# A transformer-like double block on one core: putting the square of each residual tile right behind its add

## The reference, cut to what matters

```python
y = jnp.concatenate([y_ssm, y_fft, y_att], axis=-1) @ w_out[l]
x = x + gt_m * rms_norm(y, g_post_mix[l])          # end of part 1
h = rms_norm(x, g_pre_ffn[l]) * (1.0 + sc_f) + sh_f
up = dwconv3(h @ w_up[l], conv_w[l], conv_b[l])
gate, val = jnp.split(up, 2, axis=-1)
y = (jax.nn.gelu(gate) * val) @ w_down[l]
x = x + gt_f * rms_norm(y, g_post_ffn[l])          # end of part 2
...
mix = jnp.einsum("btd,de->bte", merged, w_out[l])
h = h + rms_norm_2(mix, norm_mix_post[l])          # end of part 4
u = rms_norm_2(h, norm_mlp_pre[l])
hid = jnp.square(jax.nn.relu(jnp.einsum("btd,df->btf", u, w_up[l])))
m = jnp.einsum("btf,fd->btd", hid, w_down[l])
h = h + rms_norm_2(m, norm_mlp_post[l])            # end of part 5
```

## Time and profile before

| | |
|---|---|
| median of 3 runs | 2967.43 us (2966.15 to 2967.44) |
| the profiled execution | 2966.15 us |
| its span, first to last instruction | 2964.3 us |
| lies around the span | 1.85 us |
| PE busy | 2799.2 us (94%) |
| DVE, ACT, POOL busy | 1261.5, 875.9, 881.5 us |
| mean granted clock of TensorE | 0.97 of full speed |
| DMA | 246.00 MB, mean 83 GB/s |

### The profile page before, as it was taken

How to read it: one execution, slowest core, us unless ns; L and a number is a source line. 1 busy time by engine, 2 the same in 40 slices (tenths; PEclk the granted TensorE clock), 3 DMA queues, 4 the chain that set the end, 5 groups by cost and what they waited for, 6 DMA issues and landing times.

```text
span 2964.3 us, 31495 instructions
## 1 busy us (share of the span) xinstructions
PE 2799.2 (94%) x13134; PEld 2168.8 (73%) x13134; DVE 1261.5 (43%) x1580; ACT 875.9 (30%) x1312; POOL 881.5 (30%) x413
## 2 busy tenths in 40 slices
PE   6788889999999999979999999999999999999996
PEld 3656646778888888757777777677677888888885
DVE  6646622666444353463757522222553111111115
ACT  4413643432212121233545321111344111222112
POOL 1421113334333343333212111111245433333234
PEclk8999989999999999989999999999999999999998
DMA  6453245311111111223112221111322111111113
GB/s 229 172 143 107 59 172 209 116 55 57 43 50 50 50 43 50 100 86 114 50 57 96 76 72 54 48 59 54 121 92 105 59 43 50 50 50 43 50 50 135
DMA packets 86431, 246.00 MB, mean 83 GB/s; under 512 B 10769, under 2 KB 25617, under 8 KB 86289
## 3 DMA queue, kind: packets, MB, share of 16 engines
q1 hardware_dynamic: 78256, 219.25, 21.6%
q10 hardware_dynamic: 4608, 14.92, 1.3%
q0 software_dynamic: 3424, 9.81, 0.9%
HBM read 206.87 MB, written 37.07 MB: 82 GB/s over the span
## 4 chain that ended last, share of the span: by engine, by line
PE 82%; DVE 8%; ACT 3%; issue 2%; DMA 2%; POOL 2%; SPq 1%; ACTq 0%; POOLq 0%; DVEq 0%
PE ps L1309 24%; PE ps L1311 23%; PE ps L1310 23%; PE pc L1665 3%; PE pss L1615 1%; PE ps L1526 1%; PE ps L1472 1%; PE ps L1347 1%; POOL whl L2844 1%; PE pss L1278 1%; DMA adaw<-in_w_ada 1%; DVE y L1683 1%; DVE pad L1689 1%; DVE pad L1683 1%; POOL hid L2844 1%
## 5 line engine op out<-in xcount | busy, mean ns | idle before, releaser
L2844 POOL TENSOR_TENSOR whl<-wraw,whl 128x1024 fp32r<-128x1024 f32 (+1 forms) x247 | 640.3, 2594 | 1628.6 <-ACT whl L2402 1628.3
L1309 PE MATMUL ps<-act,whl 128*128 128x512 f32 x2464 | 1001.3, 406 | 48.0 <-DVE act L1683 11.8
L1311 PE MATMUL ps<-act,whl 128*128 128x512 f32 x2464 | 972.0, 394 | 0.0
L1310 PE MATMUL ps<-act,whl 128*128 128x512 f32 x2464 | 971.6, 394 | 0.0
L1309 PEld LDWEIGHTS ps<-act,whl 128*128 128x128 f32 x2464 | 468.2, 190 | 192.3 <-issue 75.1
L1310 PEld LDWEIGHTS ps<-act,whl 128*128 128x128 f32 x2464 | 469.1, 190 | 104.5 <-issue 8.6
L1311 PEld LDWEIGHTS ps<-act,whl 128*128 128x128 f32 x2464 | 467.6, 190 | 103.7
L2402 ACT ACTIVATE whl<-wraw 128x1024 fp32r<-128x1024 f32 (+1 forms) x247 | 256.4, 1039 | 432.2 <-PE ps L1311 393.6
L1309 PE MATMUL ps<-hid,whl 128*128 128x512 f32 x864 | 341.4, 395 | 5.4 <-POOL hid L2844 5.4
L1310 PE MATMUL ps<-hid,whl 128*128 128x512 f32 x864 | 338.4, 392 | 0.0
L1311 PE MATMUL ps<-hid,whl 128*128 128x512 f32 x864 | 338.3, 392 | 0.0
(11 more groups left out here) (321 smaller groups left out, 2461.9 us busy)
## 6 DMA issues: line engine op xcount, KB each, us to landing
wraw<-in_w_in SPq DMA_DIRECT2D x63, 512.0 KB, 3.5
wraw<-in_f1u SPq DMA_DIRECT2D x47, 512.0 KB, 3.5
wraw<-in_f2d SPq DMA_DIRECT2D x36, 512.0 KB, 3.5
wraw<-in_f2u SPq DMA_DIRECT2D x35, 512.0 KB, 3.4
wraw<-in_w_out SPq DMA_DIRECT2D x32, 512.0 KB, 3.5
x<-in_w_ada SPq DMA_DIRECT2D x32, 512.0 KB, 6.4
xs<-y SPq DMA_DIRECT2D x24, 512.0 KB, 6.7
x<-in_xT ACTq DMA_DIRECT2D x16, 512.0 KB, 8.6
```

The source lines that it names most:

```text
L1309: pe.matmul(PSB[g.bank][:, :], hi, src[:, 0, k, c], start=e == 0, stop=False)
L1310: pe.matmul(PSB[g.bank][:, :], hi, src[:, 1, k, c], start=False, stop=False)
L1311: m = pe.matmul(PSB[g.bank][:, :], lo, src[:, 0, k, c], start=False, stop=e == len(ks) - 1)
L2844: return g_.tensor_tensor(out, a, b, op)
```

## The change

It rewrites the loop in `residual`. Before, in half 0 the square of tile j was queued one turn after its add, the sum of tile j two turns after it, and a turn was 3.2 us of the plan's clock (2.0 the last of nine). Now the square is queued right behind its add, the sum one turn later, and a turn is 2.2 us (eight turns). In half 1 and for s = 5 the list stays as it was. No instruction is added or removed.

```diff
+        sums = []
+        for j in range(8):
+            p.put("r_add", s, half, j)
+            if final:
                 p.put("r_store", s, half, j)
                 yield 1.4
+                continue
+            b, free = p.use_sq(s, ("np", "rows2", s, half, j) if half else ("raS", s, j))
+            p.put("r_sq", s, half, j, b, free)
+            if half:
+                sums.append((j, b))
+            else:
+                p.sums.append((s, half, j, b))
+            if j:
+                p.add_sums(lambda entry: entry[2] < j)
+            yield 1.8 if half else 2.2
+            if len(sums) > 1:
+                p.put("r_sum", s, half, *sums.pop(0))
+        if final:
             return
-        sums = []
-        for j in range(9):
-            if j < 8:
-                p.put("r_add", s, half, j)
-            if half and j < 8:
-                b, free = p.use_sq(s, ("np", "rows2", s, half, j))
-                p.put("r_sq", s, half, j, b, free)
-                sums.append((j, b))
-                yield 1.8
-                if j:
-                    p.put("r_sum", s, half, *sums.pop(0))
-            elif half == 0:
-                if j:
-                    b, free = p.use_sq(s, ("raS", s, j - 1))
-                    p.put("r_sq", s, half, j - 1, b, free)
-                    p.sums.append((s, half, j - 1, b))
-                p.add_sums(lambda entry: entry[2] < j - 1)
-                yield 3.2 if j < 8 else 2.0
```

More of the change, by code:

```diff
@@ L628, in residual @@
         yield 1.2
-        if final:
-            for j in range(8):
-                p.put("r_add", s, half, j)
+        sums = []
+        for j in range(8):
+            p.put("r_add", s, half, j)
+            if final:
                 p.put("r_store", s, half, j)
                 yield 1.4
-            return
-        sums = []
-        for j in range(9):
-            if j < 8:
-                p.put("r_add", s, half, j)
-            if half and j < 8:
-                b, free = p.use_sq(s, ("np", "rows2", s, half, j))
-                p.put("r_sq", s, half, j, b, free)
-                sums.append((j, b))
-                yield 1.8
-                if j:
-                    p.put("r_sum", s, half, *sums.pop(0))
-            elif half == 0:
-                if j:
-                    b, free = p.use_sq(s, ("raS", s, j - 1))
-                    p.put("r_sq", s, half, j - 1, b, free)
-                    p.sums.append((s, half, j - 1, b))
-                p.add_sums(lambda entry: entry[2] < j - 1)
-                yield 3.2 if j < 8 else 2.0
+                continue
[11 more added lines that the diff above has]
+        if final:
+            return
         yield 1.0
```

## The result

The changed kernel takes 2990.42 us in the median (2983.91 to 2992.25, 4 runs), the kernel before 2967.43 (2966.15 to 2967.63, 4 runs): the ratio is 1.0075, with an interval of 1.0057 to 1.0092. It is slower by 0.75%. The profiled execution took 2984.79 us, 18.6 more than the 2966.15 of before; the forecast was 2984 with 17.8 more. The median lies inside the stated range of 2966 to 2993 and 0.4 us above the 2980 to 2990 that had most of the chance.

The account below looks back on a forecast made before the run. PE, busy 94% of the span, was taken as the bound. Two out-projections at +10.7 us each (+21.4) and -3.6 at s = 2 gave +17.8 on 2966.15: 2984 us, most likely 2980 to 2990, range 2966 to 2993.

Parts of the forecast that it names:

- The first stall: In each out-projection, PE arrives at `r_rows2` at 537.4 and waits 7.6 us for DVE's running sum, ready at 545.0.
- The clock behind it: After PE resumes at 545.0, `r_rows2` and two steps run at the low clock, 5.3 us allowed before `r_bc2` starts.
- The second stall: At `r_rows` of half 1 in each out-projection, PE waits 6 us for the last `nadd`, queued behind `apply`.
- the second has the same list: The out-projection at s = 4 was taken to cost the same 10.7 us as that at s = 1.
- the 2.1 us for the clock behind the second stall: Low clock at `r_rows` of half 1: 0.9 us more for it and 0.6 for each of two steps, per out-projection.
- The end of the first feed-forward: At s = 2, the last sum comes 5.9 us earlier, `diag` is held by POOL's split, and `r_bc2` gains 3.6 us.
- the 17.1 us wait shrinks to 11: Sign of a right forecast: PE's wait for DVE's `ss` sum at s = 2 falls from 17.1 to 11 us.
- R1: Rival, chance 0.10: DVE keeps up in the out-projections, the sum is ready at 537.8, the first stall vanishes; 2961 us.
- R2: Rival, chance 0.13: one stall only per out-projection; `r_rows` of half 1 comes at 563, +2.7 us each; 2968 us.
- R3: Rival, chance 0.15: ACT answers faster, the sum comes at 541, each out-projection costs 4 us less; 2976 us.
- R4: Rival, chance 0.07: full clock price, both out-projections at the upper bound of +15.5 us, no gain at s = 2; 2997 us.
- Part C: Half 1 and s = 5 keep their order, PE never waits for weights despite later splits: cost 0, else some 2 us.

## Why the prediction was right

**The first stall.** Forecast 7.6 us, measured 7.30 in both out-projections. The step that carried it was the walk of DVE's and ACT's new lists, round by round, and its round of 7.85 us was measured at 7.84. The other walk that might have been made is the plan's: turns of 2.2 us, sum ready in time. It fails since the plan's clock counts only PE's steps and knows of no queue.

What I had not separated is that two causes meet. The faster turn would have brought the sum 2.3 us forward, the new order loses that again, and PE's place moves by 7.5. The runs with one part each show it. The expectation of a later run, that the order alone would do no harm, was wrong: it costs 7 us at the old pace.

**The clock behind it.** I took `r_rows2` and two steps at the low level. The trace has `r_rows2` (1.87 us) and 4 steps, and `r_bc2` starts 8.5 us after `r_rows2`, not 7.3. This is the main part of the 1.2 us by which s = 1 came out above the forecast. At s = 4 it is 7.3, as forecast.

**The second stall.** At s = 1 the walk from `r_bc2` to the end of the last `nadd` gave 16.5 us (552.35 to 568.9), and measured are 16.4 (552.43 to 568.87). The stall is 5.9 where I had 6. At s = 4 it is 3.7. Here the step "the second has the same list" was too short: the order is the same, but `apply` has other instructions there. In the trace DVE writes the low parts as a plain TENSOR_TENSOR of 0.69 us, and POOL makes half of them, and from `r_bc2` (2219.47) to the end of that `nadd` (2233.82) it takes 14.3 us. That is not the whole of s = 4: `r_rows` of half 1 came 6.7 us later there instead of 8.6, and behind it the stretch lost 3.3 us more instead of 2.1. So the 2.1 us for the clock behind the second stall were too small, in both out-projections (2.4 at s = 1).

That the sum of the stretches is right to 0.2 us is luck: +1.2, -0.8 and -0.7 nearly cancel. The mechanism is not luck: both stalls came where they were said to, for the reason given, and three of the four came at their size. The fourth, the second stall at s = 4, is 3.7 us instead of 6.

**The end of the first feed-forward.** The last sum was forecast 5.9 us earlier. From `r_rows` to `r_rows2` it was 48.91 us and is 43.00: 5.91. Then `diag` was held, as walked, and `r_bc2` gained 3.55 where I had 3.6; the whole stretch gained 4.3. The sign "the 17.1 us wait shrinks to 11" did not come: it is 7.0 us, because PE came late, as told with PE's waits above; the sum came no earlier than forecast. The row of `diag` carries the price:

```profile
1332.23 2.62 DVE L1679 TENSOR_TENSOR diag<-ident,rcol 128x512 f32<-128x512 f32 x1
```

The Trainium skill (SBUF — State Buffer, "Who interferes with whom") has a DVE instruction with two SBUF inputs and a GpSimd instruction that reads SBUF shut each other out for the whole of an instruction. The trace agrees here too: 2.62 us against 0.69 in the kernel before. The half splits agree as well, since the add was let go with the first half (1.38 us).

**The rivals.** R1 (DVE keeps up) fell: the splits kept meeting the adds, and when the adds were taken away they met the sums. R2 fell with the second stall: `r_rows` of half 1 came 9.5 and 6.7 us later and not 2.7. R3, with the sum some 4 us earlier, fell with the first stall of 7.3 us. R4 fell on both counts: the out-projections cost 11.9 and 9.9 us and not 15.5, and s = 2 gained. Part C stands: in none of the three windows does PE wait for `whl`. What R1 said of the adds in general is not shown false, only that in this chain the split is released by the square that also releases DVE.

**The rest.** The stretches add up to 17.6 us and the profiled execution has 18.6 more. By the same marks the other 1.0 or so lies outside them: -0.9 us before the first, 0.0 between s = 1 and 2, +1.4 between s = 2 and 4, +0.6 behind the last. The medians differ by 23.0, and the four other runs of the changed kernel reach from 2983.91 to 2992.25. The second series of it had 2989.19 against 2968.91. Part of this may be the time before the first out-projection, which varies by some 8 us between profiles of kernels that are equal up to there (504.43 to 512.67); whether the change has a hand in it stays open, and with it some 5 of the 23 us.

## What to carry to other kernels

A plan that spaces work by PE's steps says where an instruction stands and not when it can run. Before tightening it, walk the queue of each slower engine through one round, with the measured held durations, and compare the round with the new spacing. If the round is longer, PE only gets to the wait sooner.

An instruction put at the head of an in-order queue, "right behind" what it depends on, makes all that is ready behind it wait too. Here the new order, with a square of 0.6 us ahead of an evacuation, made a round 1.4 us longer.

If a long instruction of one engine shuts out another engine, cutting it helped where the other one has pauses (17.1 to 14.1 to 12.4 us at s = 2) and not where it runs back to back (3.00 us either way). That the pauses are the reason is read from the traces, and no run has tried it.

## What was not expected of the hardware

Cutting POOL's splits had a small price. Two halves that met no DVE work took 2.53 us together against 2.40 for one. Over the program POOL was busy 990 us with halves and 1117 with quarters, against 881, and DVE 1209 and 1154 against 1261, all with the order of before. DVE's busy time falls by 53 and 108 us and POOL's rises by about twice that. It paid here because PE was waiting for DVE and not for POOL.

Equal stalls had unequal aftermaths. Both waits at `r_rows2` were 7.30 us; from there to `r_bc2`, the same work of six steps, it took 8.52 us at s = 1 and 7.32 at s = 4. The place does not decide it: in the same kernel again it took 8.38 and 7.58, with the odd adds on POOL 8.55 and 8.46, with half splits 8.52 and 8.76, all behind waits of 7.26 to 7.35 us. What does decide it no run has shown.
